# Six plain up chunks or four: the table UP_PLAIN and the order of VectorE's and ScalarE's work before Strassen's products

## The chip, the cores and the metric

The kernel runs on one core of a Trainium2 chip. The metric is the device time of one execution in microseconds; three runs of the kernel before are given with their median. Five engines work side by side, each through its own list of instructions in order: TensorE (PE, matmuls into PSUM banks), VectorE (DVE), ScalarE (ACT), GpSimd (POOL) and SyncE (SP), which here issues DMAs. They wait for each other by semaphores.

## What is computed

The reference is two transformer blocks in float32 over 512 tokens of width 1024: first a block with two attentions (stick-breaking and forgetting) and gates, then one with three mixers (pooling, a recurrent one, differential attention), a cross attention to a memory, and a convolutional feed-forward net. The change touches the last of these only:

```python
def conv_ffn(xn, w_up, conv_w, conv_b, w_down):     # D_FF = 2816, CONV_W = 3
    h = xn @ w_up
    a, b = jnp.split(h, 2, axis=-1)
    c = lax.conv_general_dilated(a, rhs, window_strides=(1,), padding=[(CONV_W - 1, 0)],
                                 feature_group_count=D_FF, ...) + conv_b
    return (jax.nn.gelu(c, approximate=False) * b) @ w_down
```

with xn the RMS-normed residual. Its input comes from the output projection of the cross attention ("xo"), which ends just before.

## The kernel before, in words

Every float32 product is made of three matmuls: each operand is split into a high part (a copy by ScalarE in a shorter format, `weights_high`, `h_high_low`, `t_high`, ...) and a low part (what is left, a subtraction by VectorE or GpSimd, `weights_low`, `h_low`, `second_low`, ...); high by high, low by high and high by low are added in PSUM. One line, L577, issues nearly all matmuls.

*Weights.* A stream of chunks (`STREAM` = 63 + 2 `UP_PLAIN`, each 128 x 2048) is loaded by SyncE into a ring of three slots. For each chunk ScalarE makes the high part (L1310) when the slot of the chunk two before is free, and GpSimd the low part in four instructions of 128 x 512 (L2851).

*The up projection.* The 22 tiles of 128 rows of `a` and as many of `b` are made in two ways. The first 2 x `UP_PLAIN` = 6 tiles of either are plain: six chunks, one for two tiles of `a` or of `b`, each tile 24 matmuls of 512 columns (8 blocks of k, three matmuls each). The other 16 pairs are chunks for Strassen's method (`UP` = 16): each chunk c is made of seven products f, named P1, R5, R7, P6, P2, Q4, P3, of 12 matmuls with 256 columns. Their weights are sums of quarters of w_up, which were summed in memory (`up_sums`) by DMAs with addition that ScalarE copies and GpSimd issues (L2864) in four parts, far earlier in the program. `UP_SEQ` is the order of the products: chunk 0's P1, R5, R7, P6, P2, then chunk 1's P1, R5, chunk 0's Q4, P3, chunk 1's R7, P6, P2, and so on. P6 is added onto the PSUM bank of P1, so PE waits before P6 until ScalarE has copied P1 away (`keep`, L1982, `sums<-banks`, semaphore `up_copied`). Two products make a *pair* of weight pieces; `pair_high(q)` is ScalarE's high part (L1322, 128 x 1024) and its low part is made by VectorE (`low_pair`, L2081), or by GpSimd where q % 7 is 2 or 5 (L2928, two instructions).

*The right side of the products* is the normed residual h: VectorE multiplies eight tiles by gain and inverse rms (`normed`, L2719), makes four sums of its quarters (L2736 to L2741, 128 x 1024 each, "token forms"), and for each of the seven forms ScalarE makes the high part (`high`, L1337) and VectorE the low part (`low_tokens`, L2081).

*What becomes of the outputs.* For tile m: VectorE moves `a` into the convolution's input (`to_conv`, L2635), ScalarE applies the first tap (`tap`, L1973), VectorE the two others (`conv`, L2641, L2642), ScalarE the gelu (L1956), and VectorE multiplies by rms and by `b` (`gact_plain`, L2647, L2649: this one frees the bank of `b`). For tiles 0 to 10 ScalarE then makes a high part for the down projection (`first_high_of`, L1337, `t_high`, 128 x 256), and VectorE the low part (`first_form`, in the steps that `FIRST_AT` names).

*The down projection* is also by Strassen's method: 28 products of 33 matmuls with 256 columns. Their weight pieces (128 x 1408) use the ring's slots and two others once these are free (`DOWN_SLOT`, `DOWN_FREE`: after which up product SyncE may load them; `DOWN_HI_FREE`: after which ScalarE may write the high part, `down_high`, L1328). GpSimd makes the low parts of pieces 0, 1, 4, 8, ... in four instructions (L2934), VectorE the others. Before the second form (R5) VectorE makes four low parts `second_low` and four sums (L2838).

The order on every engine is written out by hand in the blocks of `build`; the lists at the end of the plain chunks are in `@block.scalar` (from the `split_weights()` after the gelu table is loaded) and in `@block.vector` (from `to_conv(0)`). The lines that set the wait of this text:

```python
elif f == P6: pe.wait_ge(sem("up_copied"), 2 * c + 1)                    # TensorE
def first_high_of(m): ... M.wait_out(act, ("up", m, 1)) ... high(...)    # ScalarE, plain tiles
if n and UP_SEQ[n - 1][1] in (P1, P6): keep(*UP_SEQ[n - 1])              # ScalarE, n-th product
```

## Time and profile before

| | |
|---|---|
| median of 3 runs | 1273.41 us (1273.35 to 1275.58) |
| the profiled execution | 1275.03 us; its span 1273.2 us |
| mean granted clock of TensorE | 0.993 of full speed |
| busy: PE, DVE, ACT, POOL | 1236.6, 744.5, 628.2, 505.1 us |
| read from and written to memory | 203.57 MB, 62.93 MB |

All times within the execution are microseconds from the start of its span. A timeline row has an instruction's start, its duration, engine, line and operation, output <- input, and in brackets how long the engine had been idle and whom it waited for. Durations of PE overlap, since matmuls are pipelined: what counts is the distance between starts. A duration of the other engines includes what it waited for a port.

### The profile page before, as it was taken

The page shows a single profiled execution, that of the slowest core. Times are in us where ns is not written, and L with a number is a line of the kernel's source. Part 1 is how long each engine was busy: PE and PEld are TensorE (multiplying, and loading weights), DVE is VectorE, ACT ScalarE, POOL GpSimd, SP SyncE. Part 2 cuts the span into 40 slices and gives each one's busy share as a digit, 9 for nine tenths or more (in the row PEclk, how much of TensorE's full clock was granted, in tenths as well). Part 3 has the DMA queues.
Part 4 walks back from the last instruction along what each step waited for, and adds up shares of the span by engine and source line. Part 5 has one row for each costly group of instructions (what it writes and reads, how often), then busy time and mean ns, then how long its engine had stood idle before and what let it go on. Part 6 is the DMA issues. An engine that isn't in the chain of part 4 may idle for free.

```text
span 1273.2 us, 22257 instructions
## 1 busy us (share of the span) xinstructions
PE 1236.6 (97%) x9146; PEld 1036.3 (81%) x9146; DVE 744.5 (58%) x1159; ACT 628.2 (49%) x964; POOL 505.1 (40%) x400
## 2 busy tenths in 40 slices
PE   6999999999999999999997989999999999998999
PEld 5788888866778888767786758778878999998999
DVE  4360004886431175696646666437568788877963
ACT  6542434786665333453444544344345555556452
POOL 6554344132425545455342024531446222334421
PEclk9999999999999999999998999999999999999999
DMA  9935222567876783666363013951422555555454
GB/s 389 356 133 212 89 78 100 181 223 230 223 186 161 186 299 122 210 161 159 89 237 123 4 67 106 254 149 24 123 93 79 175 183 184 186 174 193 162 190 148
DMA packets 41746, 211.30 MB, mean 166 GB/s; under 512 B 5032, under 2 KB 5160, under 8 KB 28080
## 3 DMA queue, kind: packets, MB, share of 16 engines
q1 hardware_dynamic: 34272, 140.74, 31.2%
q0 software_dynamic: 4608, 28.31, 11.7%
q10 hardware_dynamic: 2768, 40.85, 8.9%
q8 instruction: 73, 1.20, 0.4%
q14 instruction: 25, 0.20, 0.1%
HBM read 203.57 MB, written 62.93 MB: 209 GB/s over the span
## 4 chain that ended last, share of the span: by engine, by line
PE 87%; DVE 6%; ACT 4%; issue 2%; POOL 1%; DMA 0%; ACTq 0%; SPq 0%; DVEq 0%
PE banks L577 86%; PE banks L584 2%; DVE arena L2211 1%; DVE arena L2208 1%; DVE arena L2213 1%; POOL weights_low L2851 1%; ACT weights_high L1310 0%; DMA arena<-in_mem 0%; ACT arena L1364 0%; DVE weights_low L2081 0%; DVE arena L2838 0%; ACT memory_high L1374 0%; DVE second_low L2081 0%; ACT arena L1566 0%; DVE arena L2164 0%
## 5 line engine op out<-in xcount | busy, mean ns | idle before, releaser
L2851 POOL TENSOR_TENSOR weights_low<-weights,weights_high 128x512 fp32r<-128x512 f32 (+1 forms) x260 | 353.7, 1389 | 470.3 <-ACT weights_high L1310 470.3
L577 PE MATMUL banks<-h_high_low,weights_high 128*128 128x512 f32 (+1 forms) x784 | 289.6, 369 | 1.7 <-ACT arena L1593 1.6
L577 PE MATMUL banks<-h_high_low,weights_low 128*128 128x512 f32 (+1 forms) x784 | 281.4, 359 | 0.0
L577 PE MATMUL banks<-h_low,weights_high 128*128 128x512 f32 (+1 forms) x784 | 281.2, 359 | 0.0
L577 PEld LDWEIGHTS banks<-h_high_low,weights_high 128*128 128x128 f32 x784 | 147.9, 189 | 31.2 <-issue 5.8
L1310 ACT ACTIVATE weights_high<-weights 128x2048 fp32r<-128x2048 f32 (+2 forms) x74 | 125.6, 1697 | 93.6 <-PE banks L577 90.6
L577 PEld LDWEIGHTS banks<-h_low,weights_high 128*128 128x128 f32 x784 | 148.0, 189 | 24.9 <-issue 2.9
L577 PEld LDWEIGHTS banks<-h_high_low,weights_low 128*128 128x128 f32 x784 | 147.8, 189 | 24.3
L577 PE MATMUL banks<-arena 64*64 64x64 f32 (+6 forms) x1800 | 118.6, 266 | 3.5 <-issue 2.0
L577 PEld LDWEIGHTS banks<-arena 64*64 64x64 f32 (+3 forms) x1800 | 86.5, 150 | 29.7 <-issue 22.9
L2928 POOL TENSOR_TENSOR weights_low<-weights,weights_high 128x512 fp32r<-128x512 f32 x32 | 48.5, 1538 | 112.6 <-ACT weights_high L1322 112.6
L1322 ACT ACTIVATE weights_high<-weights 128x1024 fp32r<-128x1024 f32 x56 | 59.0, 1057 | 35.2 <-PE banks L577 34.1
L1364 ACT ACTIVATE arena<-banks 128x256 f32<-128x256 f32 (+4 forms) x82 | 41.9, 520 | 62.5 <-PE banks L584 36.8
L2081 DVE TENSOR_TENSOR weights_low<-weights,weights_high 128x1024 fp32r<-128x1024 f32 (+1 forms) x44 | 55.8, 1268 | 15.8 <-ACT weights_high L1322 12.6
L577 PE MATMUL banks<-t_high,weights_low 128*128 128x256 f32 x198 | 56.0, 283 | 0.0
L577 PE MATMUL banks<-weights_high,h_high_low 128*128 128x256 f32 (+1 forms) x192 | 55.3, 288 | 0.3 <-ACT arena L1364 0.3
L577 PE MATMUL banks<-weights_high,h_low 128*128 128x256 f32 (+1 forms) x192 | 54.2, 282 | 0.0
L577 PE MATMUL banks<-token_sum_high,weights_low 128*128 128x256 f32 x192 | 54.2, 282 | 0.0
L577 PE MATMUL banks<-token_sum_low,weights_high 128*128 128x256 f32 x192 | 54.1, 282 | 0.0
L577 PE MATMUL banks<-weights_low,h_high_low 128*128 128x256 f32 (+1 forms) x192 | 54.1, 282 | 0.0
L577 PE MATMUL banks<-token_sum_high,weights_high 128*128 128x256 f32 x192 | 53.9, 281 | 0.0
L1347 ACT ACTIVATE sums<-xres 128x512 f32<-128x512 f32 x32 | 20.2, 631 | 68.0 <-DVE xres L2291 39.2
(404 smaller groups left out, 2876.5 us busy)
## 6 DMA issues: line engine op xcount, KB each, us to landing
weights<-in_stream SPq DMA_DIRECT2D x66, 1024.0 KB, 4.8
up_sums<-in_up POOLq DMA_DIRECT2D x16, 1024.0 KB, 9.4
weights<-up_sums SPq DMA_DIRECT2D x64, 256.0 KB, 2.9
weights<-in_up SPq DMA_DIRECT2D x48, 256.0 KB, 2.8
sums_kept<-in_down POOLq DMA_DIRECT2D x16, 704.0 KB, 7.0
arena<-in_ada SPq DMA_DIRECT2D x8, 1024.0 KB, 12.0
weights<-in_down SPq DMA_DIRECT2D x9, 704.0 KB, 4.2
weights<-sums_kept SPq DMA_DIRECT2D x9, 704.0 KB, 4.0
```

Of the source, the lines that this page charges most:

```text
L577: ins = nc.tensor.matmul(o, lhsT, rhs, start=start, stop=stop, skip_group_check=skip)
L584: ins = nc.tensor.transpose(o, i, ident[0:rows, 0:rows])
L1310: nc.scalar.activation(hi_of(c)[:, cols], raw_of(c)[:, cols], ACT.Copy)\
L1322: nc.scalar.activation(pair_hi(q), pair_raw(q), ACT.Copy).then_inc(sem("piece_hi"), 1)
L1347: nc.scalar.activation(SQ[n][i % 2][:, 0:width], src[:, k, 0:width], ACT.Square)\
L1364: nc.scalar.activation(dst, s_, ACT.Copy).then_inc(ring_.out(key), 1)
L2081: return tt(lo, raw, hi.bitcast(F32), ALU.subtract).then_inc(done, 1)
L2208: link(stt(w, o[:, :, 0:end], 0.0, w, ALU.max, ALU.add))
L2211: ins = nc.vector.tensor_tensor_scan(v, ones(end), v, 0.0, ALU.mult, ALU.add)
L2213: tt(w, o[:, :, 0:end], w, ALU.subtract).then_inc(M2.out(("a", i)), 1)
L2851: nc.gpsimd.tensor_tensor(lo_of(c)[:, cols], raw_of(c)[:, cols], hi_of(c)[:, cols].bitcast(F32), ALU.subtract).then_inc(sem("weights_split ...
L2928: nc.gpsimd.tensor_tensor(piece_of(pair_lo, n), piece_of(pair_raw, n), piece_of(pair_hi, n).bitcast(F32), ALU.subtract).then_inc(sem("piec ...
```

## The change

`UP_PLAIN` goes from 3 to 2: four chunks stay plain (tiles 0 to 3), and eighteen go by Strassen's method. With this the stream is two chunks shorter, the sums in memory have 18 chunks in parts of 5, 4, 5 and 4, and the slots of pairs and down pieces are dealt anew. The plain tiles use eight banks and not six. `FIRST_AT` spreads the low parts over later steps. On VectorE five tiles are normed before the first convolution and three before the second; on ScalarE and VectorE the work of tiles 4 and 5 leaves the lists before the products, and pairs, taps and token parts stand in another order.

```diff
-UP_PLAIN = 3
+UP_PLAIN = 2
...
+UP_PARTS = [slice(-(-UP * p // 4), -(-UP * (p + 1) // 4)) for p in range(4)]
...
-FIRST_AT = {2: (0, 1), 3: (2, 3), 4: (4, 5), 5: (6, 7), 6: (8, 9), 7: (10,)}
+FIRST_AT = {2: (0, 1), 3: (2, 3), 4: (4, 5), 6: (6, 7), 8: (8, 9), 10: (10,)}
...
-        PAIR_RAW_AT = [a for i in range(RAW) for a in (i and KD * F_WIDE + (i - 1) * CHUNK_F,) for a in (a, a + 2 * UP_W)]
+        PAIR_RAW_AT = [a for i in sorted(range(RAW), key=lambda i: (i - STREAM) % RAW) for a in (i and KD * F_WIDE + (i - 1) * CHUNK_F,) for a in (a, a + 2 * UP_W)]
...
-        DOWN_SLOT = [1, 2, 0, 3, 4]
-        DOWN_FREE = [104, 108, UP_N, UP_N, UP_N]
+        DOWN_SLOT = [0, 1, 2, 3, 4]
+        DOWN_FREE = [UP_N - 6, UP_N - 2, UP_N, UP_N, UP_N]
...
-        DOWN_HI_FREE = [108, UP_N, UP_N, UP_N]
+        DOWN_HI_FREE = [UP_N - 2, UP_N, UP_N, UP_N]
...
-            M.use([4, 5, 0, 1, 2, 3])
+            M.use([4, 5, 6, 7, 0, 1, 2, 3])
...
             split_weights()
-            split_weights()
             for i, f in enumerate(T_ORDER):
+                act.wait_ge(sem("token_made"), KD + {R5: 1, R7: 2, P6: 3, Q4: 4}.get(f, 0))
+                high(th_hi[f], th_raw[f], sem("token_hi"))
+                if i == 1:
+                    tap(2)
+                if i == 3:
+                    pair_high(0)
                 if i == 4:
-                    for m in range(2, 4):
-                        tap(m)
-                act.wait_ge(sem("token_made"), KD + 4)
-                high(th_hi[f], th_raw[f], sem("token_hi"))
+                    tap(3)
+            pair_high(1)
             for m in range(2, 4):
                 gelu(m)
-            split_weights()
+            pair_high(2)
             for m in range(4):
                 first_high_of(m)
-            for m in range(4, 6):
-                tap(m)
-            pair_high(0)
-            pair_high(1)
-            for m in range(4, 6):
-                gelu(m)
-            pair_high(2)
...
             to_conv(0)
-            normed(0, 1)
+            normed(0, 5)
             conv(0)
             to_conv(1)
-            normed(1, 2)
+            normed(5, KD)
             conv(1)
-            normed(2, KD)
...
+            to_conv(2)
             for m in range(2):
                 gact_plain(m)
-            for m in range(2, 4):
-                to_conv(m)
...
+            low_tokens(0)
+            to_conv(3)
+            low_tokens(1)
+            low_tokens(2)
+            conv(2)
             low_pair(0)
...
+            low_tokens(3)
+            conv(3)
+            low_tokens(4)
             low_pair(1)
...
+            gact_plain(2)
+            low_tokens(5)
+            low_tokens(6)
+            gact_plain(3)
             low_pair(2)
```

ScalarE between the last gelu of a plain tile and its copy of chunk 0's P1 (L1982, in the change L1983). Before:

```order
L1337 ACTIVATE t_high<-arena 128x256 [waits bank0_moved]
...
L1956 ACTIVATE arena<-arena 128x512 [waits conv] x2
L1322 ACTIVATE weights_high<-weights 128x1024 [waits main_filled,ada2_loaded]
L1322 ACTIVATE weights_high<-weights 128x1024 [waits main_filled,ada3_loaded]
L1982 ACTIVATE sums<-banks 128x256 [waits product_done]
```

and in the change (the banks 6, 7, 2 and 3 hold `b` of tiles 0 to 3):

```order
L1957 ACTIVATE arena<-arena 128x512 [waits conv] x2
L1323 ACTIVATE weights_high<-weights 128x1024 [waits main_filled,ada2_loaded]
L1338 ACTIVATE t_high<-arena 128x256 [waits bank6_moved]
L1338 ACTIVATE t_high<-arena 128x256 [waits bank7_moved]
L1338 ACTIVATE t_high<-arena 128x256 [waits bank2_moved]
L1338 ACTIVATE t_high<-arena 128x256 [waits bank3_moved]
L1323 ACTIVATE weights_high<-weights 128x1024 [waits main_filled,ada3_loaded]
L1983 ACTIVATE sums<-banks 128x256 [waits product_done]
```

The four high parts of tiles 0 to 3 now stand between the last gelu and the copy; before, they stood ahead of the taps of tiles 4 and 5.

VectorE in the change, from the low part of pair 0 to that of pair 3 (the two rows with `banks,arena` free banks 2 and 3):

```order
L2074 TENSOR_TENSOR weights_low<-weights,weights_high 128x1024 [waits piece_hi]
L2074 TENSOR_TENSOR token_sum_low<-arena,token_sum_high 128x1024 [waits token_hi]
L2634 SCALAR_TENSOR_TENSOR arena<-arena,params 128x512 [waits taps]
L2635 SCALAR_TENSOR_TENSOR arena<-arena,params 128x512 [waits dve_link]
L2074 TENSOR_TENSOR h_low<-h,h_high_low 128x4x256 [waits token_hi]
L2074 TENSOR_TENSOR weights_low<-weights,weights_high 128x1024 [waits piece_hi]
L2640 TENSOR_TENSOR arena<-arena,sums 128x512 [waits gelu]
L2642 TENSOR_TENSOR arena<-banks,arena 128x512 [waits main_filled,dve_link]
L2074 TENSOR_TENSOR token_sum_low<-arena,token_sum_high 128x1024 [waits token_hi]
L2074 TENSOR_TENSOR h_low<-h,h_high_low 128x4x256 [waits token_hi]
L2640 TENSOR_TENSOR arena<-arena,sums 128x512 [waits gelu]
L2642 TENSOR_TENSOR arena<-banks,arena 128x512 [waits main_filled,dve_link]
```

The gating of tile 3, the last two rows, is now behind all seven low parts of token forms; before, it stood ahead of two of them.

ScalarE at the end of the up products, before:

```order
L1982 ACTIVATE sums<-banks 128x256 [waits product_moved,product_done]
L1328 ACTIVATE weights_high<-weights 128x1408 [waits product_done,weights1_loaded]
L1973 ACTIVATE arena<-arena,params 128x512 [waits product_moved] x2
L1956 ACTIVATE arena<-arena 128x512 [waits conv] x2
L1328 ACTIVATE weights_high<-weights 128x1408 [waits product_done,weights2_loaded]
```

and in the change:

```order
L1983 ACTIVATE sums<-banks 128x256 [waits product_moved,product_done]
L1974 ACTIVATE arena<-arena,params 128x512 [waits product_moved] x2
L1957 ACTIVATE arena<-arena 128x512 [waits conv]
L1329 ACTIVATE weights_high<-weights 128x1408 [waits product_done,weights0_loaded]
L1957 ACTIVATE arena<-arena 128x512 [waits conv]
L1329 ACTIVATE weights_high<-weights 128x1408 [waits product_done,weights1_loaded]
```

The high part of down piece 0 has moved behind the last two taps and one gelu.

## Rows read from the trace of the kernel before

**Rows 1.** The page: the chain that ended last, by engine.
```profile
PE 87%; DVE 6%; ACT 4%; issue 2%; POOL 1%; DMA 0%; ACTq 0%; SPq 0%; DVEq 0%
```

**Rows 2.** The chain of waits: start, us, engine, output, line.
```profile
880.21 270.47 PE banks L577 x1814
...
1178.52 91.85 PE banks L577 x765
```

**Rows 3.** Window: length, busy PE, PEld, DVE, ACT, POOL, clock, DMA; the page's weight loads.
```profile
1020.00:1040.00 20.00, 20.00 (x172) 20.00 (x171) 18.30 (x27) 11.69 (x17) 5.67 (x4) 1.00 0.58 185
...
L577 PEld LDWEIGHTS banks<-h_low,weights_high 128*128 128x128 f32 x784 | 148.0, 189 | 24.9 <-issue 2.9
```

**Rows 4.** Timeline of VectorE: what follows plain tiles, and chunk pairs of Strassen.
```profile
899.71 0.69 DVE L2291 TENSOR_TENSOR xres<-banks,xres 128x512 f32<-128x512 f32 x1 [3.45 <-PE banks L577]
905.31 0.69 DVE L2291 TENSOR_TENSOR xres<-banks,xres 128x512 f32<-128x512 f32 x1 [1.03 <-PE banks L577]
...
1022.79 0.42 DVE L2695 TENSOR_TENSOR arena<-banks,sums 128x256 f32<-128x256 f32 x1 [0.34 <-PE banks L577]
...
1122.26 0.42 DVE L2695 TENSOR_TENSOR arena<-banks,sums 128x256 f32<-128x256 f32 x1 [0.34 <-PE banks L577]
```

**Rows 5.** The tile up_sums: GpSimd's issues, duration in ns, first and last start.
```profile
L2864 POOL DMA_DIRECT2D up_sums<-in_up x16: 760/810/1107, 304.9 to 821.2; - x16
```

**Rows 6.** Timeline of ScalarE at the start of Strassen's products.
```profile
995.83 2.01 ACT L1322 ACTIVATE weights_high<-weights 128x1024 fp32r<-128x1024 f32 x2 [3.87 <-PE banks L577]
997.75 0.37 ACT L1982 ACTIVATE sums<-banks 128x256 f32<-128x256 f32 x1
```

**Rows 7.** Timeline of VectorE beside the plain chunks.
```profile
937.26 0.74 DVE L2719 SCALAR_TENSOR_TENSOR h<-xres,params,sums 128x512 f32<-128x512 f32 x1
942.51 1.18 DVE L2641 SCALAR_TENSOR_TENSOR arena<-arena,params 128x512 f32<-128x512 f32 x1 [4.51 <-ACT arena L1973]
...
953.61 2.20 DVE L2736 TENSOR_TENSOR arena<-h 128x1024 f32<-128x1024 f32 x1
...
974.57 0.75 DVE L2642 SCALAR_TENSOR_TENSOR arena<-arena,params 128x512 f32<-128x512 f32 x1
975.24 1.22 DVE L2081 TENSOR_TENSOR token_sum_low<-arena,token_sum_high 128x1024 fp32r<-128x1024 f32 x1
976.38 1.22 DVE L2081 TENSOR_TENSOR h_low<-h,h_high_low 128x1024 fp32r<-128x1024 f32 x1
...
997.88 1.48 DVE L2081 TENSOR_TENSOR weights_low<-weights,weights_high 128x1024 fp32r<-128x1024 f32 x1 [0.53 <-ACT weights_high L1322]
```

**Rows 8.** Timeline of GpSimd: a plain chunk's low parts, and pair 2's.
```profile
953.05 8.38 POOL L2851 TENSOR_TENSOR weights_low<-weights,weights_high 128x512 fp32r<-128x512 f32 x4 [4.79 <-ACT weights_high L1310]
...
996.97 3.54 POOL L2928 TENSOR_TENSOR weights_low<-weights,weights_high 128x512 fp32r<-128x512 f32 x2 [13.42 <-ACT weights_high L1322]
```

**Rows 9.** Timeline of PE at its gaps, and windows around them (columns of rows 3).
```profile
679.12 0.49 PE L577 MATMUL banks<-h_high 64*64 64x64 f32 x8 [3.49 <-issue]
...
1175.18 0.36 PE L577 MATMUL banks<-t_high,weights_high 128*128 128x256 f32 x1 [0.75 <-DVE second_low L2081]
...
1178.52 0.47 PE L577 MATMUL banks<-t_high,weights_high 128*128 128x256 f32 x1 [2.03 <-DVE second_low L2081]
...
680.00:684.00 4.00, 4.00 (x132) 3.32 (x130) 1.91 (x6) 0.60 (x1) 1.21 (x1) 0.54 0.18 72
1176.00:1180.00 4.00, 1.97 (x12) 1.79 (x11) 4.00 (x6) 0.64 (x2) 0.00 (x0) 0.82 0.00 0
1180.00:1184.00 4.00, 4.00 (x28) 4.00 (x27) 4.00 (x5) 1.38 (x1) 2.39 (x2) 0.75 0.51 180
```

**Rows 10.** Timelines of ScalarE, GpSimd and VectorE where the up products end.
```profile
1149.34 1.38 ACT L1328 ACTIVATE weights_high<-weights 128x1408 fp32r<-128x1408 f32 x1 [1.12 <-PE banks L577]
...
1150.79 4.57 POOL L2934 TENSOR_TENSOR weights_low<-weights,weights_high 128x384 fp32r<-128x384 f32 x4 [6.10 <-ACT weights_high L1328]
...
1152.01 1.32 DVE L2641 SCALAR_TENSOR_TENSOR arena<-arena,params 128x512 f32<-128x512 f32 x1
```

28 lines of the change are left out of this document (4 added, 24 removed).

## Prediction

> **What bounds the kernel now.** I read the page first, then the chain of waits, then the stages by windows, then the timelines of single engines around the two places that the change touches. The page shows a kernel that TensorE sets: PE is busy for 1236.6 of 1273.2 us, and PE is 87% of the chain that ended last [rows 1]. The chain says more closely where: for 270.47 us from 880.21 it is PE alone, through the plain up chunks and all of Strassen's products, then come 27 us of other engines' work between the up and the down products, then PE again for 91.85 us from 1178.52 [rows 2]. So in the stretch that is edited a microsecond of PE work saved is a microsecond of time, as long as PE still never waits there; and a microsecond that PE waits is lost.
>
> A window in Strassen's part, 1020 to 1040, has 172 matmuls in 20 us with weight loading busy throughout, and VectorE busy for 18.30 of the 20 [rows 3]. VectorE is thus the engine with the least room beside PE.
>
> **The sum, step by step.** PE work. A plain up tile is 24 matmuls of 512 columns; VectorE's two residual additions that follow successive tiles of that size start at 899.71 and 905.31, so a tile is 5.60 us [rows 4]. Two plain chunks are four tiles: 22.40 us go. The two Strassen chunks that replace them are 14 products of 12 matmuls with 256 columns. Chunk pairs repeat on VectorE from 1022.79 to 1122.26, 70 products later, so a product is 1.421 us [rows 4], and 14 are 19.89 us. PE's term is **-2.51 us**. The ratio behind it is that a matmul with half the columns takes half the time (117 ns by 20 us over 171, against 233 ns by 5.60 over 24).
>
> The Trainium skill (TensorE: Matmul & The Clock Gate, section Back-to-back issue gap) speaks against that ratio: in a stream of weight loads and matmuls it measured about 81 ns for 128 columns and 131 ns for 512, so that small matmuls pay for their weight load. Between its two points my estimate for 256 columns is 98 ns, three quarters of the long one, and PE's term would be +7.0 us. The trace disagrees, and I go by the trace.
>
> DMA sums. The sums of up weights in memory grow from 16 to 18 chunks, in parts of 5, 4, 5, 4. They are made long before: GpSimd issues the last of its additions at 821.2 us [rows 5], and PE takes the first product at 995.6, or 973.2 in the change. I cost this at nothing; its cover is that gap of 150 us, and without it every extra chunk of sums would cost PE its share of a transfer.
>
> The start of Strassen's products. PE's plain work ends 22.4 us earlier, at 973.2, since it now ends at 995.6 (ScalarE sees its last tile at 995.83 [rows 6]). VectorE must by then have done its part. Laid out with the rows' durations:
> - Five norms from 937.26, some 0.67 apart, end at 940.6 in a gap where VectorE in before waits until 942.51 [rows 7]. The four moved norms save 2.7 us: with the three others and the second convolution behind, the token forms begin at 950.9, not 953.61.
> - VectorE and GpSimd hold each other up. GpSimd's four instructions from 953.05 take 8.38 us and VectorE's forms beside them, the first at 953.61, 2.2 each, where one of the same size alone takes 1.22 (1.14 to the next) [rows 7, 8]; at 997.88 one waits 0.3 us for GpSimd's first to end and then GpSimd's second waits for it [rows 7, 8]. I therefore let the two take turns, one whole instruction each, 1.1 to 1.2 us for either; instructions of VectorE that read PSUM beside GpSimd keep their 0.69 and take no turn.
> - So the four forms and GpSimd's last plain chunk interleave until 961.2. From there VectorE has no idle time: seven lows of tokens and pairs at 1.14, the input of tile 3 at 0.6 and convolutions 2 and 3 at 1.44 (two instructions of 0.75 that start 0.77 and 0.67 before the next) [rows 7] make 11.5 us, to 972.7; then gating of tile 2 (1.33) at 974.0 and a low at 975.1. GpSimd's low of pair 2 (asked for at 974.57: ScalarE's high at 973.43, 1.14 later, as at 995.83 and 996.97 [rows 6, 8]) now takes its turns, so the last low ends at 977.6 and the gating of tile 3 at about **980.0** (between 978.2 with one turn less and 980.5).
>
> What waits for that gating is the point of the sum. ScalarE's queue now has the high parts of tiles 0 to 3, the last of which waits for bank 3, that is for this gating, then the high of pair 3, and only then the copy of product P1 of chunk 0. In before the same copy stood at 997.75, 2.2 us after PE's first Strassen product began, with nothing late before it [rows 6]. Now it comes at 980.0 + 0.4 + 1.0 + 0.4 = 981.7. P6 of chunk 0 adds onto P1's bank and waits for the copy. PE reaches P6 after three products, at 973.2 + 3 x 1.42 = 977.4. It waits until 981.7: **+4.3 us** (2.5 to 4.9). All else that chunk 0 and 1 need (pair 3's low at 982.8, wanted by the seventh product) is there in time, and PE, which sets the pace behind, never gets this back.
>
> The clock. PE restarts at 1178.52 after idle gaps of 0.75 and 2.03 us, and the granted clock is 0.82 from 1176 to 1180 and 0.75 from 1180 to 1184 [rows 9]. With levels of 2.4 and 1.2 GHz that is 1.4 and 2.0 us at the lower one, 3.4 in all, and some 1.6 us of PE's work lost. After the gap of 3.49 us before 679.12 the window from 680 to 684 had it at 0.54 [rows 9], so it was low for most of 5 us after the restart. A gap of 4.3 us should bring it down too; part of the low time may pass inside the gap. I take **+1.3** (0.6 to 2.2).
>
> The turn to the down products. Down piece 0's high waits now for product UP_N-2 instead of UP_N-4, and stands behind one gelu. In before it ran at 1149.34, GpSimd split the piece from 1150.79 to 1155.36, in time for PE's first down product [rows 10]. Now high is at 1154.1 to 1155.5 (in before's times) and GpSimd's first quarter at 1156.5: PE waits 1.7 us there. But GpSimd is then quiet at 1152, and the convolution instruction of 1.32 us [rows 10] and the next go back to 0.75 each [rows 7], so ScalarE's later highs come 1 us sooner; and PE's later waits for VectorE, 0.75 and 2.03 us before 1178.52 [rows 9], swallow the delay: VectorE's last second form stays where it was, about 1178.5. PE arrives there without an idle gap, and the low clock after 1178.52, worth 1.6 us, may go. I take **-1.0** (-1.5 to +1.7).
>
> Sum: -2.5 + 4.3 + 1.3 - 1.0 = **+2.1 us**. Against the profiled execution's own 1275.03 us (span 1273.2) that is 1277.1; that execution is 1.6 us above the median 1273.41, so I predict 1275.5 us as the median. A change of 0.2% (2.55 us) is about what a measurement of this kernel can tell from none, so this is "the same", near its upper edge.
>
> **The rivals.**
> B, no stall. VectorE is ready sooner than I lay out, or turns are cheaper, and P1's copy comes by 977.4. That needs 4.3 us less in a chain of 23 VectorE instructions from 956.7 with no idle between them. For it speaks that in before the copy, done at 998.1 [rows 6], had 1.8 us in hand before P6 at 999.9, and that four norms come earlier; against it, that 22.4 us of cover go and only two tiles' work with them. Then only PE's -2.5 and the last term count: 1273.4 - 2.5 - 0 to 1.5 = 1269.4 to 1270.9.
> C, the down turn decides, and the other way: slower. If the highs of pieces 0 and 1 wait longer (piece 1's transfer can only begin at the last product but one and lands some 4 us later), VectorE's second forms shift with them. It decides from the point where PE's lateness at its first down product exceeds the 2.8 us of waits that swallow it. With 1.7 us lost in place of 1.0 won: 1273.4 + 2.1 + 2.7 = 1278.2.
> D, 256-column matmuls cost more than half of 512-column ones: bounded by one weight load of 189 ns each ([rows 3], the row of weight loads), 168 x 0.189 - 22.4 = +9.4, with my other terms 1287. The 172 matmuls in 20 us speak against it. It is the mechanism of the skill's back-to-back rule above.
> That the change does not do what it says has no room: the rows of the order show the products and the moved instructions.
>
> **How the numbers follow.** Forecast 0.74 (its own span 1273.5 to 1277.5, so 0.46 same, 0.25 slower, 0.03 faster if the clock is spared and the stall short), B 0.14 (0.10 faster, 0.04 same), C 0.11 (0.10 slower, 0.01 same), D 0.01 (slower). Faster 0.13, same 0.51, slower 0.36. The range runs from B's upper time, 1270.9, to C's, rounded up for the longest stall and clock, 1278.6.
>
> **What would show it.** In the changed profile: PE's first Strassen product about 22.4 us earlier relative to its first plain one; a PE wait of 3 to 5 us before the fourth product, released by ScalarE's copy to sums; that copy behind t_high highs that waited for VectorE's gating; matmuls at 213 ns behind the gap; 14 products more at 1.42 us; at the down turn a PE wait for GpSimd of about 1.7 us and no gap of 2 us before the last quarter of the second form. A wait under 1 us at P6 makes B right; PE going on late and then again waiting 2 us in the second form makes C right.

## The result, and the profile after the change

| | before | after |
|---|---|---|
| median of the first timing | 1274.49 us (6 runs) | 1280.59 us (6 runs, 1278.06 to 1282.87) |
| ratio | | 1.0057, 95% interval 1.0043 to 1.0071 |
| median of a second timing, later | 1275.35 us (32 runs) | 1279.75 us (10 runs) |
| ratio | | 1.0036, interval 1.0021 to 1.0050 |
| profiled execution: time, span | 1275.03, 1273.2 us | 1282.87, 1281.1 us |
| second profile: span | 1270.2 us | 1281.7 us |

The change makes the kernel slower, by 4.6 to 7.3 us (0.4 to 0.6%); I had said 2.1. Here and below a difference between kernels is worked out from the ratios, since the kernel before was timed again beside each group of runs; the plain medians differ from that by up to 1.2 us. Three timings hold one run far above all others (3081.3 and 1506.61 us of the kernel before, 1502.94 us of e8), which the ratios leave out. The page of the changed kernel, its first lines, the DMA total and the chain:

```profile
span 1281.1 us, 22433 instructions
PE 1235.3 (96%) x9218; PEld 1039.2 (81%) x9218; DVE 754.8 (59%) x1170; ACT 632.9 (49%) x973; POOL 501.4 (39%) x396
...
DMA packets 43860, 217.09 MB, mean 169 GB/s; under 512 B 5224, under 2 KB 5352, under 8 KB 30064
...
PE 82%; DVE 8%; ACT 4%; DMA 2%; issue 2%; POOL 1%; SPq 0%; ACTq 0%; DVEq 0%
```

PE's share of the chain has fallen from the 87% of [rows 1] to 82%, and 2% of the chain is now DMA, where before had 0%. PE's busy time hardly moved (1236.6 before), and its mean granted clock is 0.993 as before. So two things are to be found: what is in the chain in place of PE, and where in the execution the clock was low.

The chain of waits of the changed kernel around the start of Strassen's products (columns: start, us, engine, output, line):

```profile
980.23 2.23 DVE h_low L2074
982.46 1.69 DVE arena L2640
984.15 0.02 issue
984.17 0.70 DVE arena L2642
984.88 0.02 issue
984.90 0.02 ACT t_high L1338
...
985.22 1.04 ACT weights_high L1323
986.26 0.28 ACT sums L1983
986.54 0.04 issue
986.58 13.52 PE banks L578 x92
```

This is the stall that I forecast, link by link: gating of tile 3 (L2640, L2642), the high of its tile, the high of pair 3, the copy of P1, then PE. The edited stretch began 5.1 us later in this execution, so 984.87, the end of the gating, answers to the forecast 980.0 at 979.7. Two of VectorE's instructions are stretched while GpSimd works on pair 2: 2.31 us for a low of tokens that takes 1.22 alone, and 1.75 us for a gating product that takes 0.68:

```profile
979.02 1.22 DVE L2074 TENSOR_TENSOR token_sum_low<-arena,token_sum_high 128x1024 fp32r<-128x1024 f32 x1
980.15 2.31 DVE L2074 TENSOR_TENSOR h_low<-h,h_high_low 128x1024 fp32r<-128x1024 f32 x1
982.38 1.75 DVE L2640 TENSOR_TENSOR arena<-arena,sums 128x512 f32<-128x512 f32 x1
...
979.70 3.89 POOL L2915 TENSOR_TENSOR weights_low<-weights,weights_high 128x512 fp32r<-128x512 f32 x2 [13.31 <-ACT weights_high L1323]
```

That is the taking of turns that I had assumed. The Trainium skill (SBUF — State Buffer, section SBUF: two separate sides) calls the ports that these two share an exclusive lock held for the whole instruction, and the trace agrees: each of the two is 1.1 us longer than alone.

PE's wait at this place, and four windows of 4 us around it (columns of rows 3):

```profile
986.58 0.58 PE L578 MATMUL banks<-token_sum_high,weights_high 128*128 128x256 f32 x1 [3.87 <-ACT sums L1983]
```

```profile
980.00:984.00 4.00, 2.71 (x23) 2.50 (x22) 4.00 (x3) 0.54 (x2) 3.59 (x2) 1.00 0.97 321
984.00:988.00 4.00, 1.42 (x6) 1.42 (x7) 2.54 (x4) 2.58 (x4) 0.00 (x0) 0.63 0.16 61
988.00:992.00 4.00, 4.00 (x21) 4.00 (x20) 0.73 (x1) 1.33 (x2) 1.05 (x1) 0.52 0.34 86
992.00:996.00 4.00, 4.00 (x36) 4.00 (x35) 2.32 (x4) 1.33 (x2) 1.49 (x2) 1.00 0.43 149
```

From 988 to 992 PE is busy all the time and begins 21 matmuls, where the next 4 us have 36: the granted clock is at its lower level, 1.2 GHz, for nearly all of it. Matmuls start 213 ns apart there, as forecast.

The surprise stands further up. The chain of the changed kernel at 454 us, and at 664 us:

```profile
454.88 4.21 PE banks L578 x18
...
459.25 19.05 DMA weights<-in_stream
...
478.38 1.93 ACT weights_high L1311
480.30 0.07 issue
480.37 1.29 POOL weights_low L2838
481.67 0.14 issue
481.80 8.32 PE banks L578 x34
```

```profile
673.63 2.19 issue
675.82 0.83 PE banks L578 x6
...
678.76 1.06 PE banks L578 x56
679.83 5.03 issue
684.86 4.63 PE banks L578 x136
```

In the chain of the kernel before the first of these places is one unbroken piece of PE. At the second, "issue" means that PE waited for nothing that the trace shows; before had such a gap too, 3.49 us [rows 9].

To add up where time went I compare starts of the same VectorE instructions: up to the plain chunks the two programs are the same on that engine. Against the first profile of the kernel before, the changed kernel is late by 1.3 us from the first loads on, by another 1.2 at 40 us, wins 1.5 at 304 us (before had 3.4 us at the lower clock there, and this execution none), loses 0.9 at 480 us, 3.2 between 656 and 760 us, and stands at +5.1 where the plain chunks begin. From there to the end it loses 2.7.

### The profile page after: what moved, and what is told of

The parts are those of the page before. It is cut to its first block, busy times and chain, and to the rows that moved or that the text cites. A ratio compares the mean times of both kernels' runs of the same rounds, so it can differ in the third digit from the quotient of the medians.

```text
span 1281.1 us, 22433 instructions
## 1 busy us (share of the span) xinstructions
PE 1235.3 (96%) x9218; PEld 1039.2 (81%) x9218; DVE 754.8 (59%) x1170; ACT 632.9 (49%) x973; POOL 501.4 (39%) x396
## 4 chain that ended last, share of the span: by engine, by line
PE 82%; DVE 8%; ACT 4%; DMA 2%; issue 2%; POOL 1%; SPq 0%; ACTq 0%; DVEq 0%
PE banks L578 81%; PE banks L585 2%; DMA weights<-in_stream 1%; DVE arena L2204 1%; ACT weights_high L1311 1%; POOL weights_low L2838 1%; DVE arena L2201 1%; DVE arena L2206 1%; DVE h_low L2074 1%; DMA arena<-in_mem 0%; DVE weights_low L2074 0%; DVE arena L2640 0%; DVE second_low L2074 0%; DVE arena L2825 0%; DMA weights<-in_down 0%
## 5 line engine op out<-in xcount | busy, mean ns | idle before, releaser
L2838 POOL TENSOR_TENSOR weights_low<-weights,weights_high 128x512 fp32r<-128x512 f32 (+1 forms) x252 | 341.1, 1384 | 459.8 <-ACT weights_high L1311 459.8
L578 PE MATMUL banks<-h_high_low,weights_high 128*128 128x512 f32 (+1 forms) x816 | 298.7, 366 | 1.7 <-ACT arena L1594 1.6
L578 PE MATMUL banks<-h_high_low,weights_low 128*128 128x512 f32 (+1 forms) x816 | 290.3, 356 | 0.0
L578 PE MATMUL banks<-h_low,weights_high 128*128 128x512 f32 (+1 forms) x816 | 290.3, 356 | 0.0
L1323 ACT ACTIVATE weights_high<-weights 128x1024 fp32r<-128x1024 f32 x63 | 66.6, 1057 | 37.3 <-PE banks L578 37.1
L2074 DVE TENSOR_TENSOR weights_low<-weights,weights_high 128x1024 fp32r<-128x1024 f32 (+1 forms) x49 | 62.4, 1274 | 15.6 <-ACT weights_high L1323 12.6
L578 PE MATMUL banks<-token_sum_high,weights_high 128*128 128x256 f32 x216 | 61.4, 284 | 3.9 <-ACT sums L1983 3.9
L578 PE MATMUL banks<-token_sum_high,weights_low 128*128 128x256 f32 x216 | 61.5, 285 | 0.0
L578 PE MATMUL banks<-token_sum_low,weights_high 128*128 128x256 f32 x216 | 61.4, 284 | 0.0
L2157 DVE COPY arena<-banks 128x256 f32<-128x256 f32 (+3 forms) x40 | 25.2, 631 | 47.1 <-PE banks L578 46.1
```

Source lines behind the costliest of these rows:

```text
L578: ins = nc.tensor.matmul(o, lhsT, rhs, start=start, stop=stop, skip_group_check=skip)
L1323: nc.scalar.activation(pair_hi(q), pair_raw(q), ACT.Copy).then_inc(sem("piece_hi"), 1)
L2074: return tt(lo, raw, hi.bitcast(F32), ALU.subtract).then_inc(done, 1)
L2157: nc.vector.tensor_copy(dst, o if src is None else src(o)).then_inc(ring_.out(key), 1)
L2838: nc.gpsimd.tensor_tensor(lo_of(c)[:, cols], raw_of(c)[:, cols], hi_of(c)[:, cols].bitcast(F32), ALU.subtract).then_inc(sem("weights_split ...
```

## The experiments

My theory had two parts by now. One, recorded before: the copy of P1 is queued behind a wait for VectorE. The other, new: the larger sums in memory, which I had costed at nothing. Rivals: PE would wait there for another reason; the upstream losses are variation.

**e1_copy_first**, the changed kernel with two roundings put behind the copy:

```diff
-            for m in range(4):
+            for m in range(2):
                 first_high_of(m)
...
                 for c, f in step:
...
+                    if i == 0 and f == P2:
+                        for m in range(2, 4):
+                            first_high_of(m)
```

> The changed kernel with ScalarE's rounding of the last two plain tiles (first_high_of(2), (3)) put behind its copy of product P1 of chunk 0 instead of before the Strassen loop. Theory 1 (that copy, queued behind a wait for VectorE's gact_plain(3), causes PE's 3.87 us stall at product P6 of chunk 0, and the stall causes the 6.8 us at the lower clock after it): the stall falls below 0.5 us, the granted clock stays at 1.00 from there to the last up product, and the time is 4.0 + 2.65 = 6.6 us below the changed kernel, about 1274 us, level with the kernel before. Rival (VectorE is late anyway, and its next product, P2 or the first tap, makes PE wait in its place): a stall of 2 to 4 us a few products later, the low clock stays, and the time is 0 to 2 us below the changed kernel. Rival 2 (the clock falls at this place for another reason): only the 4.0 us come back, 1276.5 us.

**e2_before_18_sums**, the kernel before with sums of the changed kernel's size:

```diff
+SUM_UP = UP + 2
+SUM_PARTS = [slice(-(-SUM_UP * p // 4), -(-SUM_UP * (p + 1) // 4)) for p in range(4)]
...
-                return v[UP // 4 * p:UP // 4 * (p + 1)]
+                return v[SUM_PARTS[p]]
...
-    up_sums = nc.dram_tensor("up_sums", [4, UP, P, UP_W], F32, kind="Internal").ap()
+    up_sums = nc.dram_tensor("up_sums", [4, SUM_UP, P, UP_W], F32, kind="Internal").ap()
```

> The kernel before, with its DRAM-to-DRAM sums made over eighteen up chunks in parts of 5, 4, 5 and 4 instead of sixteen in parts of 4; the two added chunks are duplicates that nothing reads, and all else is as before. Theory 1 (the 3 to 5 us that the changed kernel has lost before the up projection begins are the price of the longer copies and adds, through idle time of PE between 656 and 690 us and smaller delays earlier): 3 us (2 to 5) above the kernel before, about 1277.5, with an idle stretch of some 5 us of PE near 685 us. Rival (those microseconds are variation from one execution to the next, or come from elsewhere): within 0.7 us of the kernel before.

**e3_after_16_sums**, the reverse; the sums of the last two chunks are left out, so this kernel is for timing alone:

```diff
-UP_PARTS = [slice(-(-UP * p // 4), -(-UP * (p + 1) // 4)) for p in range(4)]
+UP_PARTS = [slice(4 * p, 4 * (p + 1)) for p in range(4)]
...
-                sp.dma_start(piece_of(pair_raw, n), up_from[f][c]).then_inc(pair_loaded(q)[0], 16)
+                sp.dma_start(piece_of(pair_raw, n), up_from[f][c] if c < 16 else up_in[A11][c]).then_inc(pair_loaded(q)[0], 16)
```

> The changed kernel with its DRAM-to-DRAM sums made over sixteen chunks in parts of 4, as in the kernel before; for the last two chunks the sums are left out, and their pieces are read from the input A11 instead, at the same time and in the same size. Theory 1 (the larger sums cost the time upstream): 3 us (2 to 5) below the changed kernel, about 1277.5 us, and the up projection begins 0 to 1 us from where it began before. Rival (they cost nothing): within 0.7 us of the changed kernel, 1280.6 us.

**after_again** has no edit.

> The changed kernel once more, for a second profile. Theory 1 (the offsets between the two profiles ahead of the up projection belong to the program): the idle stretch near 685 us and the offset of 3 to 5 us at the first plain product come again, and so does the 3.9 us stall at product P6 of chunk 0. Rival (variation from one execution to the next): the offset at the first plain product is below 2 us in this profile, with the idle stretches elsewhere, and only the stall at P6 comes again. Time 1280.6 (1278 to 1283) by both.

Measured, with the kernel before at 1275.35 us on this chip:

| | median, runs | ratio to before, interval | span of its profile |
|---|---|---|---|
| e1_copy_first | 1274.46 (12) | 0.9995 (0.9983 to 1.0008) | 1275.0 |
| e2_before_18_sums | 1277.74 (12) | 1.0020 (1.0009 to 1.0031) | 1276.0 |
| e3_after_16_sums | 1278.71 (9) | 1.0025 (1.0012 to 1.0039) | 1273.4 |
| after_again | 1279.75 (10) | 1.0036 (1.0021 to 1.0050) | 1281.7 |

e1 is 0.41% below the changed kernel, 5.2 us, near the 6.6 of theory 1 and outside both rivals (0 to 2, and 4.0) by its median, though their distance from 4.0 is within the noise. The trace decides: PE's wait at P6 is now of another kind and a seventh of the size, and the window that had 0.52 has the full clock.

```profile
987.75 0.39 PE L578 MATMUL banks<-token_sum_high,weights_high 128*128 128x256 f32 x1 [0.57 <-DVE sums L2678]
```

```profile
988.00:992.00 4.00, 4.00 (x36) 4.00 (x36) 2.80 (x5) 1.70 (x2) 0.16 (x1) 1.00 0.50 159
```

e2 is 2.6 us (1.1 to 4.0) above the kernel before: the sums do cost, about what theory 1 said, though the idle stretch near 685 us was 2.8 us and not 5. e3 answers less clearly, 1.4 us below the changed kernel (1.0 by the medians) where 3 was expected, with intervals that overlap, and its plain chunks began 2.8 us earlier than before's, not 0 to 1 us from them. In after_again all came again that theory 1 named: 3.7 us idle up to 682.86, plain chunks 5.5 us late, the stall of 3.87 us. What was wrong in the expectation is that I had taken single profiles for the size: spans of one kernel differ by some 3 us here from one execution to the next. What is the same in each profile is the place. At 480 us PE waits 0.8 to 1.7 us for weights_low in all six further profiles that have eighteen-chunk sums and the S2 copies where they were (e1, e2, the second of the changed kernel, and later e4, e6 and e7), and in none with sixteen. ScalarE's rounding of that weight chunk shows why, in the kernel before and in e2:

```profile
474.62 1.92 ACT L1310 ACTIVATE weights_high<-weights 128x2048 fp32r<-128x2048 f32 x1 [3.05 <-DMA weights<-in_stream]
```

```profile
477.92 1.92 ACT L1312 ACTIVATE weights_high<-weights 128x2048 fp32r<-128x2048 f32 x1 [6.64 <-DMA weights<-in_stream]
```

The chunk lands 3.3 us later in this pair, which is an extreme one: six profiles with sixteen-chunk sums have the start of this rounding at 474.6 to 476.2 us, seven with eighteen at 476.4 to 478.4, so 1.9 us later in the mean. What is larger is the copies of S2 out of S1 that are issued just ahead of it (two of the four parts have 1,280 KB in place of 1,024). That they delay it is so far an inference; a run below moves copies and tests it. And at 674 to 686 us the gaps put down to "issue" come again: 2.2 and 5.0 us in the changed kernel, 1.2 and 3.7 in its second profile, 1.7 and 5.6 in e1, 1.7 and 2.8 in e2; 3.5 in the kernel before, 2.9 in e3.

Why "issue"? In this stretch the tiny 64 x 64 matmuls of the differential heads run, up to 400 in 10 us where plain stretches have 40; and the S4 copies run beside them. PE must be given its instructions, and the profile lists queues of kind "instruction". The DMA view of 8 us of the changed kernel, 674 to 682, and of 10 us of a kernel shown further below (e6), 674 to 684, whose copies are elsewhere:

```profile
q10 hardware_dynamic: 101, 2.21, 79.1%
q1 hardware_dynamic: 42, 0.34, 13.2%
q14 instruction: 1, 0.01, 0.4%
```

```profile
q1 hardware_dynamic: 85, 0.57, 13.4%
q8 instruction: 3, 0.05, 2.0%
```

q10 carries the copies and has 79% of all 16 engines; in those 8 us no packet of q8 begins. Microsecond by microsecond of the trace, q8's packets of the changed kernel begin in 661, 673, 682, 686, 690 us, and PE's gap ends at 684.86; in e6 they come every 3.3 to 5.2 us from 670 to 728 us.

Two things in the traces tie the gaps to these packets. The seventeen profiles of this text have 34 idle stretches of PE of over 1 us by "issue" from 656 to 750 us, and every one ends 1.2 to 1.6 us after a packet of q8 has ended (1.38 in the kernel before, 1.43 for the 5.03 us of the changed one). And they fall at eight places of PE's program only, behind 7,423, 7,673, 7,925, 8,177, 9,437, 10,693, 10,947 and 11,201 matmuls and weight loads: 250 to 254 apart, or five times that. By these figures PE stops where a packet's worth of its instructions is used up; for the 5.03 us the next packet began 2.7 us after PE had stopped. So the new theory: PE's next instructions come late because their packets stand behind those of the copies. Then moving the copies must move the gaps.

**e4_copy_first_s4_later** and **b1_before_s4_later** move the S4 copies to steps 10 to 13, the first on e1, the second on the kernel before, with the same edit:

```diff
             for i in range(4):
                 diff_tick(i)
                 dv_out(4 + i, 5 + i)
-                for n in (2 * i, 2 * i + 1):
-                    later_copies(S4, S2, n, 3)
...
             diff_tick(10)
+            for n in (0, 1):
+                later_copies(S4, S2, n, 3)
```

and so on behind steps 11, 12 and 13. **e5_all_moved** is e4 with the S2 copies of the down sums moved too:

```diff
-                later_copies(S2, S1, m, 2)
+                if m < 4:
+                    later_copies(S2, S1, m, 2)
                 if m % 4 == 3:
                     split_weights()
+            for m in range(4, KD):
+                later_copies(S2, S1, m, 2)
```

> The version with ScalarE's copy of P1 ahead of the two roundings (e1_copy_first), and the eight DRAM-to-DRAM copies that begin the sums S4 moved on ScalarE's queue from the first four steps of the differential heads (656 to 674 us, where the profiles show PE idle with nothing to wait for but its own instructions) to steps 10 to 13 (some 722 to 742 us), a stretch in which the DMA engines move next to nothing. Theory 1 (PE's idle time of 1.7 and 5.6 us at 674 and 684 us is the time in which its next instructions, fetched by a DMA queue of their own, stand behind the copies' packets): both idle stretches shrink below 1 us together, the lower clock at 686 us goes or is halved, and the time is 5 us (3 to 8) below e1_copy_first, about 1269.5 us, below both kernels. Rival (the idle time belongs to that code, with or without copies): the gaps stay and the time is within 0.7 us. Rival 2 (the copies do the same harm wherever they stand): gaps of 2 to 5 us appear near 725 to 750 us instead, and the time is within 1.5 us.

> The kernel before with nothing changed but the same move of the eight copies that begin S4. Theory 1: the 3.49 us gap at 679 us and the 6.8 us of lower clock behind it go, 3.5 to 7 us below the kernel before, about 1270 us. Rival (the gap belongs to that code): within 0.7 us of the kernel before. If this gains less than the same move in the changed kernel, the difference is what the eighteen-chunk copies cost there.

> e4_copy_first_s4_later, and the four copies of the down sums S2 moved behind the loop over the merged tiles instead of every second one inside it (ScalarE, 462 to 471 us). Theory 1 (the third weight chunk of that stage lands 3.6 us late behind the larger copies, and PE waits 1.1 to 1.7 us for POOL's weights_low at 480 us): that wait goes, 1.5 us below e4. Rival (the copies of the up sums, which stay, are what delays that chunk, or the moved copies delay the next chunks as much): within 0.7 us of e4, or slower by up to 2 us with a new wait at 485 to 500 us.

> The kernel before once more, for a second profile. If the places of its lost time belong to the program, the idle stretch of PE near 679 us (3.5 us) and the lower clock behind it come again, and there is no wait above 0.9 us at 480 us; the low clock at 304 us, which one of four later profiles has, may or may not come. Time within 0.3 per cent of the kernel before.

Measured, before at 1273.18 us (29 runs): e4 1279.87 (6 runs), ratio 1.0047 (1.0032 to 1.0063); b1 1278.03 (12), 1.0031 (1.0017 to 1.0045); e5 1276.78 (12), 1.0025 (1.0013 to 1.0036); before_again 1272.94 (10), 0.9997 (0.9981 to 1.0013).

My times were wrong by 8 to 10 us, and the mechanism was right. Rival 2 of e4 holds, and more strongly than I had put it: e4 is 0.52% or 6.6 us above e1, where that rival allowed 1.5. (By its profile, which is the fastest of its six runs, it is 0.8 us above.) Of e4, PE's idle time of over 0.9 us by "issue" from 656 to 750 us:

```profile
697.78 0.38 PE L578 MATMUL banks<-arena 128*128 128x128 f32 x2 [1.05 <-issue]
...
720.34 1.97 PE L578 MATMUL banks<-arena 64*64 64x64 f32 x119 [1.02 <-issue]
727.22 1.22 PE L578 MATMUL banks<-forget_rows,consts 128*128 128x512 f32 x1 [3.09 <-issue]
734.16 0.34 PE L578 MATMUL banks<-h_high,arena 64*64 64x64 f32 x6 [2.09 <-issue]
```

The gaps at 674 to 686 us are gone: by 690 us e4, b1 and e5 have won 5.1 to 5.2 us on the kernel before since 650 us. All of it and 3 to 4 us more is lost again between 720 and 760 us, where the copies now are. I had chosen the place by the DMA engines' load, next to nothing; it is also a place where PE issues small matmuls fast (301 between 720 and 730 us in the kernel before). What counts is how fast PE uses up its instructions while the copies run.

e5 is 0.2% below e4, 2.8 us where 1.5 was expected, with intervals that just overlap, and its wait at 480 us is gone: ScalarE rounds that weight chunk at 471.13 us in place of 474 to 478. So the copies issued ahead of that chunk are what delays it; a9, b8 and e8 below show the same, at 470.3 to 471.6 us.

before_again shows the gap near 679 us smaller and in pieces (1.58, 0.60, and 0.77 to 0.84 three times by 701 us), and the lower clock there for 3.4 us in place of 6.8. The place returned, its size did not.

**e6_s4_early** and **b6_before_s4_early** put the S4 copies where PE issues some 40 matmuls in 10 us, ahead of the differential heads (on e1, and on the kernel before); **e7_s4_late** and **b7_before_s4_late** behind them, at steps 17, 18, 19 and 21. Of e6:

```diff
             dq_square(3)
+            act.wait_ge(sem("up_sums_added"), 16 * DOWN_PAIRS * 3)
+            copy_up(S4, up_sums[S2], 0)
             dq_inverse(2)
             dq_square(4)
+            copy_up(S4, up_sums[S2], 1)
...
             dq_square(6)
+            act.wait_ge(sem("sums_added"), 16 * DOWN_PAIRS * 3)
+            copy_down(S4, sums_kept[S2], 0)
             dq_inverse(5)
```

> e1_copy_first with the eight copies that begin S4 moved to 610 to 636 us on ScalarE (one behind each of eight steps of the differential queries and keys), where PE issues some 40 matmuls in 10 us, against 150 to 400 in 10 us where the copies stood and where e4 put them. Theory, mended by e4 and b1 (copies stop PE wherever it runs through its instructions fast, since the next ones arrive late behind the copies' packets; where its matmuls are long, they do not): no idle time put down to issue above 1.1 us between 656 and 750 us, the stretch from 650 to 720 us shortened by 5 us against the kernel before and by 9 us against e1_copy_first, no new wait above 2 us for a weight chunk, and the time 6 to 9 us below e1_copy_first: about 1266 us where the kernel before has 1273.5. Rival (the copies now delay the weight chunks at 604 to 641 us as they do at 480 us, and PE waits for those): 2 to 4 us come back lost there, and the time is 3 to 5 us below e1_copy_first.

> e1_copy_first with the same eight copies moved to 752 to 771 us on ScalarE, behind the last steps of the differential heads, where PE issues some 40 matmuls in 10 us and the DMA engines stand idle between 756 and 779 us. Theory: as for e6, the idle stretches go and no new ones come; 6 to 9 us below e1_copy_first. Rival (the copies run on to some 785 us, into the first weight chunks of the mixers and into GpSimd's wait for them at 793 us, on whose engine the low halves of the weights are queued): a new wait of PE of 2 to 5 us at 780 to 800 us, and the time is 2 to 5 us below e1_copy_first.

> The kernel before with the same move to 610 to 636 us as e6. Theory: 5 us (3.5 to 7) below the kernel before, and level with e6 within 1 us, since then what is left between the two is the matmuls saved (2.5 us), the shorter down turn (1 to 2 us) and the larger weight and copy traffic at 480 us (1 to 2 us). Rival (the smaller copies cost little in the kernel before): within 1.5 us of the kernel before.

> The kernel before with the same move to 752 to 771 us as e7. Theory: 5 us (3.5 to 7) below the kernel before. Rival (a new wait at 780 to 800 us): 0 to 3 us below it.

| before 1274.35 (30 runs) | median, runs | ratio, interval |
|---|---|---|
| e6 | 1267.93 (7) | 0.9960 (0.9945 to 0.9974) |
| e7 | 1270.20 (12) | 0.9973 (0.9959 to 0.9988) |
| b6 | 1270.19 (12) | 0.9970 (0.9956 to 0.9983) |
| b7 | 1270.55 (12) | 0.9977 (0.9965 to 0.9989) |

All four are faster than both kernels. e6 is 0.35% below e1, 4.5 us of the 6 to 9 expected; b6 and b7 gain 3.8 and 2.9 of the 5 expected, so the sizes were again a quarter to 40% too high; I had taken them from profiles with large gaps. By the times alone e6 and e7 (4.5 and 2.8 us below e1) would fit their rivals, 3 to 5 and 2 to 5 us; the waits that these rivals name are not in the profiles, which lose nothing against e1 or before from 600 to 650 us (e6) and have no wait of 2 us at 780 to 800 us (e7). b6 is 1.3 us above e6, where I had said within 1. The windows of the kernel before and of e6 (columns as above):

```profile
650.00:700.00 50.00, 43.13 (x1134) 36.86 (x1136) 34.00 (x86) 22.70 (x55) 17.72 (x14) 0.93 0.54 186
```

```profile
650.00:700.00 50.00, 45.90 (x1292) 38.85 (x1294) 37.46 (x94) 26.15 (x64) 17.70 (x14) 1.00 0.14 46
```

The same 50 us hold 158 matmuls more, at the full clock. e7 has two new waits, 1.30 us for ScalarE at 750.68 and 1.24 by issue at 756.18; b7 has the same two. Each is less than the 2 to 5 us that the rival names, and they are in another place.

Last, whether these two places are all of the upstream loss. **a9_change_copies_moved** is the changed kernel, stall and all, with both moves (those of e6 and e5); **b8_before_copies_moved** the kernel before with both; **e8_both_and_copy_first** e6 with the move of e5.

> The changed kernel, with its stall at product P6 of chunk 0 left as it is, and both groups of copies moved: S4's to 610 to 636 us as in e6, the four copies of the down sums S2 behind the loop over the merged tiles as in e5. Theory (what the change loses before the up projection is all due to its larger copies, in these two places): against b8, the kernel before with the same moves, only the edited region is left, +2.7 to +3.0 us by the profiles (matmuls -2.5, stall and clock +6.5, down turn -1.3), so about 1272.5 us where the kernel before has 1274; no wait above 0.9 us at 480 us and no idle stretch above 1.1 us by issue from 656 to 750 us. Rival (something else in the changed kernel costs time upstream): 5 us or more above b8.

> The kernel before with both groups of copies moved as in a9. Theory: the move of the S2 copies gives nothing here, since the profiles of the kernel before show no wait at 480 us with sixteen chunks; so as b6, 3.8 us (1.8 to 5.6) below the kernel before. Rival (the copies cost there too, unseen): 1 us or more below b6.

> e6_s4_early with the four S2 copies moved as well: the changed kernel without its stall and with both groups of copies out of the way. Theory: the wait of 0.8 to 1.7 us at 480 us goes, some 1.2 us below e6 and 6 us below the kernel before, about 1267.5 us where that has 1274; against a9 the 6 us of stall and clock, 5 us (4 to 6.5) below it; against b8 the matmuls saved and the shorter down turn alone, 2 to 3 us below it. Rival (one of these gains is taken by another wait): within 0.7 us of e6.

| before 1274.09 (18 runs) | median, runs | ratio, interval | span |
|---|---|---|---|
| a9 | 1270.91 (11) | 0.9978 (0.9970 to 0.9987) | 1269.1 |
| b8 | 1268.25 (5) | 0.9963 (0.9950 to 0.9976) | 1263.4 |
| e8 | 1267.47 (7) | 0.9948 (0.9928 to 0.9969) | 1265.8 |

a9 is 0.15% above b8, 1.9 us (2.7 by the medians) where the edited region alone should leave 2.7 to 3.0, and the rival's 5 or more is out. In a9 nothing waits at 480 us, issue gaps from 656 to 750 us stay under 0.9 us, and the stall is there unchanged:

```profile
974.59 0.58 PE L578 MATMUL banks<-token_sum_high,weights_high 128*128 128x256 f32 x1 [3.87 <-ACT sums L1994]
```

e8 is 3.8 us below a9 (4 to 6.5 expected), and 1.9 below b8 (2 to 3 expected; 0.8 by the medians). b8 has five runs only. It gains 4.7 on the kernel before; b6 had 3.8, so the S2 move gave the sixteen-chunk kernel nothing that can be told from noise. e8 is the fastest version measured, 6.6 us (3.9 to 9.2) below the kernel before; against e6 its 1.5 us lie within both intervals.

## Why the prediction was wrong, step by step

Time from the start of the plain chunks to the end, by the spans of the profiles less the offset at 880 us, sets the steps of the edited region apart from all that lies ahead:

| profiles | us from 880.21 of the kernel before to the end of the span |
|---|---|
| sixteen Strassen chunks: before twice, e2, b1, b6, b7, b8 | 391.5 to 394.1, mean 392.9 |
| the change, stall in: after twice, e3, a9 | 395.7 to 396.0, mean 395.9 |
| the change, stall out: e1, e4, e5, e6, e7, e8 | 390.1 to 391.2, mean 391.0 |

- **The whole region, +2.1 in the sum**: 395.9 - 392.9 = +3.0 in the profiles, +1.9 (2.7 by the medians) by the times of a9 and b8. Right to about 1 us, in part by luck, since the stall was sized too long and the clock's part too short.
- **The stall, +4.3**: 3.87 us in each of the four profiles that have it (3.88 in e3), with each link of its chain. Right, 0.4 us shorter than forecast, and rival B is out.
- **The clock, +1.3**: with levels of 2.4 and 1.2 GHz, the granted 0.63 and 0.52 of the two windows are 3.0 and 3.8 us at the lower one, in one piece from 985.0 to 991.8. From PE's restart at 986.58 that is 5.2 us, in which 2.6 us of work are lost: the mechanism was right, the term too small, and its upper end of 2.2 too. a9 has the same; in the second profile and in e3 the low time was 3.4 us, which makes 1.7. Stall and clock together are 395.9 - 391.0 = 4.9 us by the profiles, 3.8 (e8 against a9) and 5.2 (e1) by the times, for 5.6 in the sum.
- **PE's work, -2.51**: PE's first Strassen product begins 115.4 us behind the point at 880.21 before and 93.0 in the change, the 22.4 us that I had laid out. The products take 159.2 us before; in the change they take 185.6 with stall and clock and 179.1 without, 19.9 more: -2.5. Right, and rival D is out. What I did not foresee: in six profiles (after_again, e3, e4, e5, e7, e8) all these matmuls start 119.2 ns apart at the full clock, in the other eleven 118.5, in all some 1.0 us over the 1,512 of them. No trace shows why. It takes back 0.6 us of the saving in the mean of the ten changed profiles.
- **The down turn, -1.0**: from the end of the up products to the end of the span 118.5 us before and 117.2 in the change, -1.2. PE's first wait was 1.72 us. The profile puts it down to VectorE, which had ended at 1165.06; GpSimd's first quarter of the piece ends at 1165.63 and PE begins at 1165.73, so it is the wait that I had laid out. No gap of 2 us came behind, and what is won is the low clock: the sixteen-chunk profiles take some 118.4 or 119.5 us with 3.4 or 6.8 us of it there, and 116.9 or 117.0 without (b7, b8); the changed ones take 117.2, and e1, with 3.4 us of it, 118.0. Rival C, which would have added 1.7, is out. The table agrees: stall out against sixteen chunks, 391.0 - 392.9 = -1.9, is -1.5 for PE's work with the loss just named, +0.6 for the wait that is left at P6, and -1.0 for the turn.
- **The DMA sums, 0**: this is the step that failed. "I cost this at nothing; its cover is that gap of 150 us" asked only when the sums must be done. It did not ask what their transfers delay on their way, half a kernel earlier: the same program with only the sums enlarged (e2) is 2.6 us slower, 1.1 to 4.0. The two places are a weight chunk at 480 us and PE's own instructions at 656 to 690 us. With +2.6 in that term the sum is +4.7, or +5.6 with the region as measured, inside the +4.6 to +7.3 of the two timings. With the 1.4 us of the reverse, e3, it would be +3.5 or +4.4, just below them.

The profile of before held the sign of it. [rows 9] quote the gap of 3.49 us "issue" at 679.12; I read it only as an example of what a gap does to the clock, and did not ask what makes PE wait for nothing just where ScalarE issues 7 MB of copies. Rival times were all worked out inside the edited region, so but for D's 1287, at a chance of 0.01 and outside the range, no case reached past 1278.6.

What stays open is how the 2.6 us are shared between the two places. Between 400 and 500 us the seven profiles with large sums and S2's copies unmoved lose 0.9 to 2.2 us, 1.5 in the mean; that leaves about 1 for the instruction fetch, while the two profiles of the changed kernel lose 3.2 and 3.7 from 650 to 800 us, and e2's 1.2. The first loads' 1.3 and 1.2 us did not return in the second profile of the changed kernel (0.1): variation.

## What to carry to other kernels

A bulk transfer with slack before its data are wanted is not free: price it where it runs, by what shares the DMA engines with it in that stretch. Weight chunks are one such thing; an engine's own instructions are another, and here a gap that the profile puts down to "issue" in a stretch of many small matmuls, beside running copies, was the sign of it: see whether it ends just behind a packet of an instruction queue. Put copies where matmuls are long and few, not where the DMA engines look idle. And when work in front of a loop shrinks, look at what stands ahead of the first evacuation in the evacuating engine's queue: here two roundings behind that copy in place of ahead of it gave back 4 to 5 us.

## What the runs showed of the hardware

- PE stood still for up to 5.6 us (e1, up to 684 us) while copies between DRAM tensors ran, with 64 x 64 matmuls at up to 40 a microsecond; the packets of the instruction queue q8, regular every 3.3 to 5.2 us without the copies (e6, 670 to 728 us), were 9 us apart (673 to 682 us). Each of 34 such standstills of over 1 us ended 1.2 to 1.6 us after the end of a q8 packet (16,384 bytes), and they fell at eight places of the program, 250 to 254 matmuls and weight loads apart or five times that. Moving the copies moved the standstill with them, three times out of three (e4, b1, e5), and took it away or below 1.8 us when they went where PE issued 4 matmuls a microsecond (e6, b6, e7, b7, a9, b8, e8). What is left without copies beside it, 1.4 to 1.8 us in b6, b7 and e8, ends in the same way behind a q8 packet.
- These gaps can cost twice, as the stall did: before had the lower clock for 6.8 us, 676.8 to 683.6, around the end of its gap at 679 us, e6 and b6 not at all there. The gaps are not the only cause: e7 and a9, with no gap of 1 us before 690 us, had 3.4 us of it behind a wait of 1.7 us for ScalarE at 674.6 us.
- With copies of 1,280 KB in place of 1,024 KB in two parts of four, a 1,024 KB weight chunk on another queue was there 1.9 us later in the mean of the profiles (476.4 to 478.4 us against 474.6 to 476.2), and taking four copies of 704 KB from in front of it brought it in at 470.3 to 471.6 us (e5, a9, b8, e8).
- Matmuls of 256 columns at the full clock start 118.5 ns apart through all up products in eleven profiles and 119.2 ns apart in six; at the lower clock, 213 ns.
- Executions of one unchanged kernel differ by up to 9.4 us within one timing (1268.55 to 1277.95, the kernel before beside e6), and in the profiles part of it sits in these gaps. A difference of 2 us in one pair of profiles says nothing unless its place comes again.
